# MOBA heads: q and k turned by VectorE in 32x32 blocks in place of TensorE's transposes

## The reference

```
mq = rotary(mq.reshape(B, S, MOBA_HEADS, MOBA_HEAD_DIM), ROT_DIM, ROPE_THETA)
mk = rotary(mk.reshape(B, S, MOBA_HEADS, MOBA_HEAD_DIM), ROT_DIM, ROPE_THETA)
...
s_own = jnp.einsum('hqd,hkd->hqk', qc, k_own, preferred_element_type=jnp.float32) * scale
s_own = jnp.where((kpos[None, :] <= qpos[:, None])[None], s_own, -jnp.inf)
p = jax.nn.softmax(...)
o = ... jnp.einsum('hqk,hkd->hqd', p_own, v_own)
```

## Time and profile before

| | before |
|---|---|
| median of 3 executions | 2460.41 us (2459.68 to 2460.59) |
| profiled execution | 2460.38 us |
| its span | 2458.6 us |
| PE busy | 2451.1 us (100%) |
| DVE busy | 1525.2 us (62%) |
| ACT busy | 1233.6 us (50%) |
| POOL busy | 225.4 us (9%) |
| granted clock, mean | 1.00 |
| DMA, mean | 189 GB/s |

### The profile page before, as it was taken

How to read it: one execution, slowest core, us unless ns; L and a number is a source line. 1 busy time by engine, 2 the same in 40 slices (tenths; PEclk the granted TensorE clock), 3 DMA queues, 4 the chain that set the end, 5 groups by cost and what they waited for, 6 DMA issues and landing times.

```text
span 2458.6 us, 35621 instructions
## 1 busy us (share of the span) xinstructions
PE 2451.1 (100%) x11823; PEld 2046.3 (83%) x11823; DVE 1525.2 (62%) x1796; ACT 1233.6 (50%) x1627; POOL 225.4 (9%) x241
## 2 busy tenths in 40 slices
PE   9999999999999999999999999999999999999999
PEld 7888888878888888888888888888887888888887
DVE  5444445587876777777777776454456655555564
ACT  5445455555455444444444446454556555655443
POOL 0021224231000000000000000010000100520000
PEclk9999999999999999999999999999999999999999
DMA  7655555567655555555555556855554555544655
GB/s 262 194 180 172 173 174 175 178 229 229 211 192 176 189 192 189 189 188 188 188 188 189 189 186 212 254 183 178 168 183 163 177 166 172 179 163 161 224 186 163
DMA packets 134658, 464.23 MB, mean 189 GB/s; under 512 B 14528, under 2 KB 20928, under 8 KB 133952
## 3 DMA queue, kind: packets, MB, share of 16 engines
q1 hardware_dynamic: 122336, 443.60, 55.3%
q10 hardware_dynamic: 12256, 19.73, 2.4%
HBM read 455.93 MB, written 7.34 MB: 188 GB/s over the span
## 4 chain that ended last, share of the span: by engine, by line
PE 98%; issue 1%; DVE 1%; ACT 0%; DMA 0%; POOL 0%; ACTq 0%; POOLq 0%; DVEq 0%
PE PS L629 21%; PE PS L631 21%; PE PS L630 21%; PE PS L858 13%; PE PS L861 7%; PE PS L884 3%; PE PS L885 3%; PE PS L883 3%; PE PS L728 1%; PE PS L670 1%; PE PS L711 1%; PE PS L691 1%; PE PS L736 0%; PE PS L719 0%; DMA CONST<-constants 0%
## 5 line engine op out<-in xcount | busy, mean ns | idle before, releaser
L1565 DVE TENSOR_TENSOR WL<-RAW,WH 128x1024 fp32r<-128x1024 f32 x842 | 1058.9, 1261 | 875.9 <-ACT WH L1065 871.0
L1065 ACT ACTIVATE WH<-RAW 128x1024 fp32r<-128x1024 f32 x842 | 890.8, 1060 | 1119.1 <-PE PS L631 733.4
L629 PE MATMUL PS<-WH,HT 128*128 128x512 f32 (+1 forms) x1816 | 721.0, 397 | 0.2
L631 PE MATMUL PS<-WH,HT 128*128 128x512 f32 (+1 forms) x1816 | 707.0, 389 | 0.0
L630 PE MATMUL PS<-WL,HT 128*128 128x512 f32 (+1 forms) x1816 | 705.7, 389 | 0.0
L629 PEld LDWEIGHTS PS<-WH,HT 128*128 128x128 f32 x1816 | 341.1, 188 | 72.4 <-issue 6.1
L631 PEld LDWEIGHTS PS<-WH,HT 128*128 128x128 f32 x1816 | 340.8, 188 | 71.5
L630 PEld LDWEIGHTS PS<-WL,HT 128*128 128x128 f32 x1816 | 341.5, 188 | 66.8
L858 PE MATMUL PS<-HT,WH 128*128 128x512 f32 x1408 | 384.7, 394 | 0.0
L858 PEld LDWEIGHTS PS<-HT,WH 128*128 128x128 f32 x1408 | 241.1, 189 | 32.6
L861 PEld LDWEIGHTS PS<-HT,WL 128*128 128x128 f32 x1408 | 216.3, 189 | 30.1
(11 more groups left out here) (288 smaller groups left out, 1908.9 us busy)
## 6 DMA issues: line engine op xcount, KB each, us to landing
RAW<-w_stream SPq DMA_DIRECT2D x842, 512.0 KB, 3.4
bias_scratch<-BE ACTq DMA_DIRECT2D x12, 256.0 KB, 3.9
X<-x_in SPq DMA_DIRECT2D x4, 512.0 KB, 7.6
MEMR<-mem_in ACTq DMA_DIRECT2D x1, 2048.0 KB, 9.6
X<-x_in ACTq DMA_DIRECT2D x4, 512.0 KB, 4.1
x_scratch<-X ACTq DMA_DIRECT2D x4, 512.0 KB, 4.0
X<-x_scratch ACTq DMA_DIRECT2D x1, 2048.0 KB, 8.8
out<-X ACTq DMA_DIRECT2D x8, 256.0 KB, 3.3
```

The source lines that it names most:

```text
L629: pe.matmul(o, hi, WH[:, slot, kk, 0:cols], start=k == 0, stop=False)
L631: ins = pe.matmul(o, lo, WH[:, slot, kk, 0:cols], start=False, stop=k == nq * GK - 1)
L1065: act.activation(WH[:, g.slot(j)], RAW[:, g.slot(j)], ACT.Copy).then_inc(hi_split, 1)
L1565: dve.tensor_tensor(WL[:, s], RAW[:, s], WH[:, s].bitcast(F32), ALU.subtract).then_inc(lo_split, 1)
```

## The change

GpSimd's wait before head 0 is for four products (q and k) in place of six. TensorE's and ScalarE's `head_transpose` leave the MOBA heads. VectorE does the turn in two halves, after its splits of steps 0 and 1 of each head: `moba_turn(H, 0)` and `moba_turn(H, 2)`, eight `transpose` instructions each. One instruction takes a 32-partition quarter a and a 32-column stripe b of q and k of both token tiles (2 x 2 x 32 = 128 elements a partition), transposes the 32x32 blocks and writes them to quarter b of QKT. The last raises `qk_tr`. TensorE waits for `qk_tr` in step 3, raises `qkt_ready` itself and goes on to the scores; its wait for `head_out` stands in step 7, ahead of the transposes of the output, which share bank 5.

```
-            hold(prod_free, 2 + 6)
+            hold(prod_free, 2 + 4)
...
             def moba_step(i, p):
                 for r in range(2):
                     h = i * 2 + r
-                    st = head_steps(MOBA, At(MOBA0 + r, i, 2), lambda s: MQKV[:, s, ds(h * P + 2 * W, P)], (2, 3, 5, 6, 7))
+                    H = At(MOBA0 + r, i, 2)
+                    st = head_steps(MOBA, H, lambda s: MQKV[:, s, ds(h * P + 2 * W, P)], (None, 3, 5, 6, 7))
+                    if p - 8 * r == 3:
+                        pe.wait_ge(qk_tr, H.count(2))
+                        pe.sem_inc(qkt_ready, 1)
+                    if p - 8 * r == 7:
+                        pe.wait_ge(head_out, H.count(1))
...
-                    st = head_steps(MOBA, At(MOBA0 + r, i, 2), At(r, i, 2), i * 2 + r, None, (2, 3, 5, 7))
+                    st = head_steps(MOBA, At(MOBA0 + r, i, 2), At(r, i, 2), i * 2 + r, None, (None, 3, 5, 7))
...
+            def moba_turn(H, a0):
+
+                dve.wait_ge(qk_fixed, H.count(1))
+                for a in (a0, a0 + 1):
+                    for b in range(4):
+                        src = QK[32 * a:32 * a + 32, :, :, 32 * b:32 * b + 32]
+                        dst = QKT[32 * b:32 * b + 32, :, 0, :].rearrange("p z (t s) -> p z t s", t=T)[:, :, :, 32 * a:32 * a + 32]
+                        ins = dve.transpose(dst, src)
+                if a0:
+                    ins.then_inc(qk_tr, 1)
...
                     split(At(GROUP0["ret_proj"], i, 2 * GD), p + RING)
                     for r in range(2):
-                        st = head_steps(MOBA, At(MOBA0 + r, i, 2), At(r, i, 2), i * 2 + r, None, (3, 6, 7))
+                        H = At(MOBA0 + r, i, 2)
+                        if p - 8 * r in (0, 1):
+                            moba_turn(H, 2 * (p - 8 * r))
+                        st = head_steps(MOBA, H, At(r, i, 2), i * 2 + r, None, (3, 6, 7))
```

## The result

The changed kernel takes 2465.52 us (median of 13, 2464.74 to 2465.95) against 2460.41 (median of 13, 2459.62 to 2460.88): 5.1 us slower, a ratio of 1.0021 with the interval 1.0013 to 1.0028. The forecast was 2466.3.

The account below looks back on a forecast made before the run. TensorE, with 98% of the chain that ended last, was taken as the bound: 4.35 us saved against 10.2 us of waits before the scores gave 2460.4 + 5.85 = 2466.3 us, range 2459 to 2471.5 (8 in 10).

Parts of the forecast that it names:

- The gain: TensorE without the q and k transposes: 3.29 us from heads 1 to 7 plus 1.06 in head 0, at most 4.35 us.
- The early start's share: Head 0: GpSimd's wait for four products lets TensorE regain the 0.59 us lost waiting for its last rotation instruction.
- The price of one transpose: VectorE, start to start: 0.30 us long plus a 0.03 gap, 0.333 us, without overlap; bounds 0.21 and 0.37.
- the first rival: VectorE's transposes overlap at 0.21 us each, so TensorE never waits before the scores: 2456.1 us, chance 0.15.
- The date: q and k lie turned 7.69 us after step 0's split starts; scores late by 1.63 (head 0), 0.82 (odd), 1.31 (even).
- The restart: TensorE before the scores in each head: 0.12 us of restart plus 0.05 for the weight load, on top of the lateness.
- What was costed at nothing: ScalarE's lost copies, TensorE's moved output wait and own semaphore, later splits, loads and masks: 0 us at the end.
- The second rival: VectorE's short transposes cost 0.37 us each, adding 0.59 us a head, 4.7 in all: 2471.0 us, chance 0.13.
- the cover theory: VectorE has half its time free, so the turn is ready before TensorE asks: like the first rival or near 2460, chance 0.05.
- the fourth: Rival for head 0: GpSimd's early start does nothing, as the turn comes last; 0.59 us regained and lost again, no chance given.

Follow-up runs that it names:

- the pairs: The changed kernel with each transpose cut in two of 64 elements (q, then k), both from and to the same quarter, 32 instructions a head: 2477.89 us.
- the late start: The changed kernel with GpSimd again waiting for all six products before head 0, in place of four: 2468.3 us.

## Why the prediction was right

**The gain.** 4.35 us was worked out, 4.14 measured by the balance (7 x 0.45 and 1.03 in place of 7 x 0.47 and 1.06). The early start's share, 0.59, was 0.63 in the medians when run alone.

**The price of one transpose.** The duration, 0.30 us from 1024 elements scaled down, was right to 3 ns. The distance, 0.333, was 0.315: I had added a gap of 0.03, seen around the long ones, and 0.012 was there. That the lengths don't overlap where quarters change is what decided the sign. With the mean distance of 0.215 that the run without the change of quarter had, head 0's chain is 5.97 us, just under its date of 6.06, and the time was 2456.8, the first rival's 2456.1 but for 0.7. By the Trainium skill (page "VectorE: DVE Perf Modes", section "Two Vector instructions with no wait between them") an instruction that reads or writes from another quarter than the last one did starts only when the earlier ones have finished. Both runs agree: 0.303 long and every 0.315 with the change, every 0.19 at a length of 0.26 without it, and in the pairs every second one overlaps.

**The date.** Chain 7.69 forecast, 7.44 measured. The lateness of the turn is the end of the last transpose against the last L631 plus 0.23: 1.38, 0.56 and 0.97 in heads 0, 1 and 2, forecast 1.63, 0.82 and 1.31.

**The restart.** This term was mis-sized: 0.17 forecast, taken from a wait for another engine in front of other instructions. The scores cost 1.76, 0.82 and 1.35 us above their 0.66, so 0.38, 0.26 and 0.38 on top of the lateness: from the last transpose to the first L711 0.15 to 0.28 us, and 0.57 instead of 0.46 from L711 to the next L629. Two errors of opposite sign: eight times 0.25 to 0.34 too much lateness, 0.1 to 0.2 too little restart. Losses 10.2 forecast, 9.19 measured.

**What was costed at nothing.** The moved wait of TensorE was not free: 0.44 us over the eight heads. ScalarE's lost copies, the late splits, loads and masks were. The second rival (0.37 a transpose) and the cover theory fell with the trace; the fourth was right, in that head 0's regained 0.59 was lost again.

**The sum.** -4.14 + 9.19 + 0.44 = +5.49, against +5.85 forecast; the medians differ by 5.1. The mechanism was right head by head; that the total came so close is in part luck, since 1.0 us too much loss stands against 0.2 too much gain and 0.44 left out.

The Trainium skill's rule (page "VectorE: DVE Perf Modes", section "Rules for kernel authors") that leaves a 128x128 transpose to TensorE gave the right sign for this placement and the wrong one for the exchange as such: with the turn ahead of the split, VectorE's 40 us of transposes are hidden whole and 4.0 us are gained, some 0.6 of them by GpSimd's early start.

## What to carry to other kernels

When work is moved from the bound engine to an idle one, compute the date at which its last instruction ends, with everything that stands between in that engine's queue, and compare it with the step that needs it; the mean load says nothing. Here one split of 1.25 us between the two halves turned 3 us of gain into 5 us of loss. Put the work where the helper engine would otherwise stand idle, and before anything with a deadline further off; but then see to it that its own inputs are there, since what is queued behind waits too.

## What the runs showed of the hardware that was not expected

In the stage of the change TensorE's granted clock fell after long waits and only then. After waits of up to 1.53 us before L711 (head 0 of the changed kernel 1.50, the odd heads of the kernel with pairs 1.53) the matmuls came every 0.23 us again from the third on. In the kernel with pairs, whose four even heads waited 2.04 to 2.46 us, it fell after three of them (heads 0, 2 and 6), for some three to six matmuls every 0.43 us; head 4, with 2.09 us, came through at 1.00 while head 6, with 2.04, did not, so near there it is not decided by the length alone. After 3.31 us (the late start) seven came every 0.43, the stretch's clock 0.73: the lower level, 1.2 GHz, for part of it. Each of these four falls cost 1.6 us on top of the wait. The same happened at the start of two programs: behind a wait for the constants of 1.94 and 2.07 us (the turn ahead of the split with the late start, and the turn left out) the granted clock of 8 to 12 us was 0.59 and 0.58. There the waits alone do not sort the profiles, though: the kernel before and the changed one, with 1.68 and 1.57 us, ran the matmuls behind the wait at half rate too (L670 every 0.21 us in place of 0.11), and so already the last one ahead of it (0.63 us long in place of 0.45), while 1.84 us left the clock at 1.00 elsewhere. Where exactly it begins was not measured.

GpSimd's instructions and VectorE's splits held each other up. An instruction of GpSimd's rotation lasts 0.32 us when alone; each of the 111 in the twelve traces that began inside a split, with over 0.15 us of it left, ended 0.18 us after that split's end. The other way round, each of the 173 splits from 90 to 346 us that began with over 0.16 us of a GpSimd instruction still to run ended 1.07 to 1.09 us after that instruction: 1.42 us in place of 1.23 beside L484, 1.75 beside L508. So each of the two engines can delay the other without a semaphore between them: this is the 0.5 us of head 7's output step above, and the 0.9 us by which head 0's rotation was longer in the kernel before than with the late start.
